# Delta rule block inverse: products on the changed half of the columns, with T1 kept in a zero-padded tile per level

## The reference, cut to what matters

```python
lower = eye + beta[..., :, None] * einsum('...id,...jd->...ij', k, k) * dec_strict
solve = partial(lax.linalg.triangular_solve, left_side=True, lower=True, unit_diagonal=True)
u  = solve(lower, beta[..., None] * v)
wk = solve(lower, (beta * exp(gc))[..., None] * k)
...
w = u_c - wk_c @ state
o = qd_c @ state + qk_c @ w
state = gl_c * state + swapaxes(kd_c, -1, -2) @ w
```

## Time and profile before

| what | value |
|---|---|
| runs | 5391.55, 5387.68, 5394.68 us |
| profiled execution | 5387.88 us, span of its instructions 5386.1 us |
| mean granted PE clock | 0.961 of 2.4 GHz |
| busy: PE, PEld, DVE, ACT, POOL | 4440.8, 2253.3, 3353.6, 1396.1, 2775.4 us |
| ten preparations (five steps, two layers) | 149.79 us |
| ten runs of levels 1 to 6 | 388.94 us |
| ten ends of a step | 122.26 us |

### The profile page before, as it was taken

One profiled execution on the slowest core, in us unless ns is written; L12 is line 12 of the kernel. 1 busy time (PEld: TensorE's weight loads), 2 busy tenths in 40 slices (PEclk: granted clock), 3 DMA queues, 4 the chain that ended last, 5 costly groups with the idle time before them and its releaser, 6 DMA issues. The chain is left out here.

```text
span 5386.1 us, 51105 instructions
## 1 busy us (share of the span) xinstructions
PE 4440.8 (82%) x15092; PEld 2253.3 (42%) x15092; DVE 3353.6 (62%) x8542; ACT 1396.1 (26%) x3530; POOL 2775.4 (52%) x2690
## 2 busy tenths in 40 slices
PE   8788899788878878777697888987988788887775
PEld 3488664433323323222245886643333233332222
DVE  5455474666666666766465554746666666666664
ACT  1221453222222222222202114522222222222221
POOL 0022100577777777777600220007777777777775
PEclk9888899999999999999998888998999999999999
DMA  7100001899999999999860000029999999999998
GB/s 248 39 3 1 16 1 55 331 409 409 409 405 404 404 400 398 399 398 399 351 237 13 3 1 16 1 72 378 409 409 409 406 405 403 396 403 391 386 395 317
DMA packets 425563, 1471.60 MB, mean 273 GB/s; under 512 B 46528, under 2 KB 52288, under 8 KB 424768
## 3 DMA queue, kind: packets, MB, share of 16 engines
q0 software_dynamic: 368640, 1342.34, 63.2%
q1 hardware_dynamic: 56640, 125.89, 6.6%
HBM read 1464.49 MB, written 3.57 MB: 273 GB/s over the span
## 5 line engine op out<-in xcount | busy, mean ns | idle before, releaser
L1525 PE MATMUL psall<-ring,diag 128*128 128x512 f32 x5120 | 2483.2, 614 | 674.5 <-DMA ring<-in_peer_v,eidx 555.6
L1337 DVE CUSTOM_DVE_ANT_0 ring<-ring,mixed 128x1024 f32<-128x1024 f32 x1280 | 1565.0, 1223 | 1013.8 <-DMA ring<-in_peer_u,eidx 1013.3
L1256 POOL DMA_INDIRECT ring<-in_peer_u,eidx x1280 | 1285.1, 1004 | 1136.8 <-DVE eidx L1194 747.0
L1525 PEld LDWEIGHTS psall<-ring,diag 128*128 128x128 f32 x5120 | 888.1, 190 | 2225.2 <-DMA ring<-in_peer_v,eidx 1472.8
L1256 POOL DMA_INDIRECT ring<-in_peer_v,eidx x1280 | 1313.6, 1026 | 411.9 <-issue 262.8
L1422 ACT ACTIVATE act<-dot 128x2 f32<-128x2 f32 x640 | 130.2, 203 | 2269.7 <-DVE dot L1337 2269.7
L1414 ACT ACTIVATE diag<-cons,wgt 128x128 f32<-128x128 f32 x1280 | 443.1, 393 | 209.6 <-DVE wgt L1317 207.5
L464 POOL TENSOR_TENSOR mlt<-lt,lmask 128x512 f32<-128x512 f32 x120 | 174.5, 1464 | 471.2 <-DVE lt L550 333.1
L1481 PE MATMUL psall<-h2T,wq 128*128 128x128 f32 (+1 forms) x1024 | 285.9, 434 | 1.3 <-DVE x L1299 1.3
L456 POOL MEMSET state<- 64x512 f32 x2 | 1.0, 518 | 502.0 <-POOLq L375 502.0
L1481 PEld LDWEIGHTS psall<-h2T,wq 128*128 128x128 f32 x1024 | 157.7, 191 | 132.4 <-issue 130.7
(11 more groups left out here) (285 smaller groups left out, 4851.0 us busy)
## 6 DMA issues: line engine op xcount, KB each, us to landing
mixed<-in_w_mod SPq DMA_DIRECT2D x32, 1024.0 KB, 5.4
wq<-in_w_pq SPq DMA_DIRECT2D x64, 512.0 KB, 6.8
ring<-in_peer_u,eidx POOLq DMA_INDIRECT x1280, 11.7
ring<-in_peer_v,eidx POOLq DMA_INDIRECT x1280, 11.7
wring<-in_w_mod SPq DMA_DIRECT2D x8, 2048.0 KB, 14.4
wring<-in_w_in_tm SPq DMA_DIRECT2D x4, 2048.0 KB, 12.5
ring<-in_w_out SPq DMA_DIRECT2D x4, 2048.0 KB, 11.4
wring<-in_w_in_fm SPq DMA_DIRECT2D x2, 2048.0 KB, 8.4
```

The source lines that it names most:

```text
L1256: nc.gpsimd.indirect_dma_start(out=ring[:, n % slots, :], out_offset=None, in_=d[table], in_offset=bass.IndirectOffsetOnAxis(ap=p.eidx[:, ...
L1337: nc.vector.tensor_tensor_reduce(out=p.u[:, n % UR, :], in0=p.u[:, n % UR, :], in1=p.mixed[:, t, :], scale=1.0, scalar=0.0, op0=ALU.mult, ...
L1525: mm = nc.tensor.matmul(bank, p.diag[:, n % VR, :], p.v[:, n % VR, 512 * c:512 * c + 512], start=(s == 0), stop=(s == UNIT - 1))
```

## The change

At a level with blocks of b = 2^lvl columns, only one of every two neighbouring blocks of columns changes. The new helper `joined` takes these blocks alone as a strided access pattern (runs of b, every 2b), 64 columns of 128; `packed` is the same count without gaps. T1, both products and both subtractions now work on 64 columns a head: T1 goes packed into columns 0 to 255 of bank 0, XT' T1 into columns 256 to 511 of bank 0, T1' XT into columns 0 to 255 of bank 1. T1' XT needs T1 as the stationary operand at full width. So ACT writes T1 into the right columns of a tile `t1z`, of which there is one for each direction and level, zero elsewhere; POOL clears all twelve once per layer, in front of its first mask, and ACT waits for that once per direction and layer. The number of matmuls, the order of the work and the waits are otherwise the same. No transfer is touched.

```diff
+    def joined(ap, lvl, side):
+        return ap.rearrange("p (g s b) -> p g s b", s=2, b=2 ** lvl)[:, :, side, :]
+    def packed(ap, lvl):
+        return ap.rearrange("p (g b) -> p g b", b=2 ** lvl)
+    def flat(ap):
+        return ap.rearrange("p h n -> p (h n)")
...
             nc.gpsimd.memset(p.state[:, :, :, :], 0.0).then_inc(sem("states_zero"), 1)
+            nc.gpsimd.memset(p.t1z[:, :, :, :], 0.0).then_inc(sem("t1_zero"), 1)
...
                         if n >= 1:
                             act.wait_ge(sem(f"t2{d}"), n)
-                        nc.scalar.activation(p.t1s[:, d, :], ps[4 * d][:, :], ACT.Copy).then_inc(sem(f"t1s{d}"), 1)
+                        else:
+                            act.wait_ge(sem("t1_zero"), 1)
+                        nc.scalar.activation(joined(p.t1z[:, d, lvl - 1, :], lvl, d), packed(ps[4 * d][:, 0:256], lvl),
+                                             ACT.Copy).then_inc(sem(f"t1s{d}"), 1)
...
                         if lvl < LEVELS - 1:
-                            nc.vector.tensor_tensor(p.X[:, d, :, :], p.X[:, d, :, :], heads(ps[4 * d][:, :]), ALU.subtract).then_inc(sem(f"x{d}"), 1)
-                        nc.vector.tensor_tensor(p.XT[:, d, :, :], p.XT[:, d, :, :], heads(ps[4 * d + 1][:, :]), ALU.subtract).then_inc(sem(f"x{d}"), 1)
+                            x = joined(flat(p.X[:, d, :, :]), lvl, d)
+                            nc.vector.tensor_tensor(x, x, packed(ps[4 * d][:, 256:512], lvl), ALU.subtract).then_inc(sem(f"x{d}"), 1)
+                        x = joined(flat(p.XT[:, d, :, :]), lvl, 1 - d)
+                        nc.vector.tensor_tensor(x, x, packed(ps[4 * d + 1][:, 0:256], lvl), ALU.subtract).then_inc(sem(f"x{d}"), 1)
...
-                            mm = nc.tensor.matmul(B[0][:, h * P:(h + 1) * P], p.mlt[:, d, lvl_buf(n), h, :],
-                                                  p.X[:, d, h, :], start=True, stop=True)
+                            mm = nc.tensor.matmul(packed(B[0][:, h * 64:(h + 1) * 64], lvl), p.mlt[:, d, lvl_buf(n), h, :],
+                                                  joined(p.X[:, d, h, :], lvl, d), start=True, stop=True)
...
-                                nc.tensor.matmul(B[0][:, h * P:(h + 1) * P], p.XT[:, d, h, :],
-                                                 p.t1s[:, d, h * P:(h + 1) * P], start=True, stop=True)
+                                nc.tensor.matmul(packed(B[0][:, 256 + h * 64:256 + (h + 1) * 64], lvl), p.XT[:, d, h, :],
+                                                 joined(p.t1z[:, d, lvl - 1, h * P:(h + 1) * P], lvl, d), start=True, stop=True)
...
-                            mm = nc.tensor.matmul(B[1][:, h * P:(h + 1) * P], p.t1s[:, d, h * P:(h + 1) * P],
-                                                  p.XT[:, d, h, :], start=True, stop=True)
+                            mm = nc.tensor.matmul(packed(B[1][:, h * 64:(h + 1) * 64], lvl), p.t1z[:, d, lvl - 1, h * P:(h + 1) * P],
+                                                  joined(p.XT[:, d, h, :], lvl, 1 - d), start=True, stop=True)
...
-                    p.t1s = sb(c3, "t1s", [P, 2, HC * P])
+                    p.t1z = sb(c3, "t1z", [P, 2, LEVELS - 1, HC * P])
```

## The result

The changed kernel takes 5665.66 us (median of four runs, 5651.65 to 5670.07) against 5393.11 us for the kernel before, a ratio of 1.0498 with a 95% interval of 1.0472 to 1.0525: slower by 273 us. The profiled execution took 5670.07 us at a mean granted clock of 0.903 (before 0.961).

The account below looks back on a forecast made before the run. PE's pace was taken to carry most of a level's time, DVE's the rest, with the granted clock deciding. 5387.9 + 227 (levels) + 31.5 (ends) = 5646, or 5650 against the median; forecast 5648 us, range 5605 to 5672.

Parts of the forecast that it names:

- Weight loads set PE's pace: Matmuls in the levels: 64 columns save PE nothing; 0.111 us each at full clock, 0.214 at half; 61.6 us a step.
- the second rival: Delta steps: the clock returns in four of the ten, each giving back 28.7 us; 5531 us, chance 0.06.
- the first rival: Levels: the clock stays at or returns to 2.4 GHz, saving 29 us in all; 5359 us, chance 0.06.
- The clock does not return: From the start of the levels to the step's end, the clock stays at 1.2 GHz in all ten steps; chance 0.86.
- The rival with four steps that recover: Four of ten delta steps keep an early clock rise, each giving back 28.7 us; 5531 us, chance 0.06.
- The rival in which the clock stays up: Levels at 2.4 GHz: a level takes 5.65 us in place of 6.17; 5359 us, chance 0.06.
- the ends: End of each delta step, at half clock: 15.4 us against a mean of 12.2, +31.5 us over ten.
- ACT, DVE and POOL: Levels: L504 falls to 390 to 400 ns, L579 and L580 to about 420; POOL's clearing of about 6.2 us is covered.
- the rival's sum: Levels at full clock with shorter DVE terms: 2.9 us saved a step, 29 in all, giving 5359 us; chance 0.06.
- the level term: Level parts: 288 matmuls at 0.214 us make 61.6 us a step in place of 38.9, +227 over ten.
- the preparations: Start of each delta step: no change on the mean, up to 7 us either way over ten.

Follow-up runs that it names:

- the first experiment: The changed kernel with all matmuls of the levels at 128 columns again, ACT and DVE at half, against the kernel before: 5374.11 us, ratio 0.9969.

## Why the prediction was right

*Weight loads set PE's pace: right.* 61.6 us a level part was forecast, 62.09 measured. At half clock the pace is 1.71 / 8 = 0.214 us with 64 columns, at full clock 0.89 a group with 64 as with 128. The Trainium skill ("TensorE: Matmul & The Clock Gate", section "LDWEIGHTS (loading the stationary operand)") gives a load's time as columns over 1.2 and names no clock, an estimate of 107 ns for 128 columns; that comes near the 0.111 us at full clock (0.89 / 8) and not the 0.214 at half, and the measurement decides. Where the prediction says that by the page the second rival's time would follow, the sum meant can only be the first rival's, 5359, in which half clock costs PE nothing.

*The clock does not return: right, in all ten steps.* The rival with four steps that recover had 0.06; those steps too read 0.50 from the first level to the end. The rival in which the clock stays up is real, only not for this kernel: with T1 full at levels 1 to 3 it gives 5363 where its sum was 5359, and a level of 5.58 where 5.65 was worked out. That the two times lie so near is in part luck: the level parts gave about 30 us of the 29 forecast, the ends some 12 more that were not in the sum, and the span outside the stage was 19 us longer. The rule of the Trainium skill ("TensorE: Matmul & The Clock Gate", section "Part 1: The HAM clock gate (the "warmup" mystery)") that sustained matmul activity brings the full clock does not hold here if activity is read as a busy PE: 61 us of unbroken work stayed at half clock.

*ACT, DVE and POOL: right, and worth nothing here.* The groups of the first step, and the clearing:

```profile
L595 DVE TENSOR_TENSOR XT<-XT,psall 128x256 f32<-128x256 f32 x12 | 5.0, 415 | 5.7 <-PE psall L685 5.7
L516 ACT ACTIVATE t1z<-psall 128x256 f32<-128x256 f32 x12 | 4.6, 387 | 53.8 <-PE psall L664 53.8
L593 DVE TENSOR_TENSOR X<-X,psall 128x256 f32<-128x256 f32 x10 | 4.2, 420 | 40.1 <-PE psall L685 40.1
...
248.22 5.21 POOL L466 MEMSET t1z<- 128x6144 f32 x1
```

DVE now waits 40.1 us for PE ahead of X alone. The shorter operations pay only where the clock is up: 28.5 us over ten level parts in the first experiment, against the 29 of the rival's sum.

*The sum.* 258.5 us were forecast for the stage, 264.2 came: the level term was 5.0 short, the ends 1.4, the preparations 0.6 over. The level term took all 288 records as T1 and products; 16 of them are kT' state, which has 64 rows and had 64 columns already. At level 2 it alternates with T1, and these four groups take 7.53 us (291.53 to 299.06) in place of 4 x 1.712 = 6.85, about 0.7 us a step; the other groups come out a little under 1.71. The other 18 us of the profiled span lie outside the delta stage. They do not follow the change: outside the stage the nine traces of this case take 4716 to 4753 us, 4725 in the kernel before, 4743 in the changed kernel, and the least in the changed kernel with the unused matmuls. What they are stays open. In the medians the difference is 272.6. For the same reason the prediction's premise that the stage passes its gain or loss to the end one for one holds only to within about 25 us: in the first experiment the stage is about 42 us shorter (28.5 in the levels, the rest in the ends and preparations) and the time 18.6.

## What to carry to other kernels

Before narrowing a matmul, look at what sets its pace: where the rows show the same time for 64 and for 128 moving columns, half the columns save nothing on PE. Then look at the granted clock where the narrowed work begins. Here it began at half clock, the wide matmuls were what brought the clock back, and without them the whole stage stayed down. In such a place narrow the copies out of PSUM and the vector work, and leave the matmuls wide, at least the first ones behind a wait.

## What was not expected

Sixteen unused matmuls a step, meant to start the levels at full clock, made the kernel before 60 us slower: they moved the half-clock stretch from level 1, where PE's wait for DVE hid it, into level 2, where 10.88 us at 0.54 were on the path. And 64-column matmuls of the levels were seen to go on at either clock: at 0.50 for 61 us in the changed kernel, at 1.00 for the 14.96 us of levels 4 to 6 with T1 full before them.
